# Gated mixer of a two-layer decoder: gate chains beside one value unit each, the last unit of r behind the core, head products and lower parts taking turns, the output's first unit tile by tile

## The reference, cut to what matters

```python
def gla_mixer(h, w_in, w_g2, b_g, head_norm, w_out):
    q, k, v, g_lr, r = _split(h @ w_in, ODD_SPLITS)
    gk = jax.nn.log_sigmoid((g_lr @ w_g2 + b_g).astype(jnp.float32)) / GLA_TAU
...
    G = jnp.cumsum(chunks(gk, GLA_DKH), axis=3)
    G_last = G[:, :, :, -1:, :]
    q_dec = q * jnp.exp(G)
    k_inv = k * jnp.exp(-G)
    k_rem = k * jnp.exp(G_last - G)
    att = jnp.where(tril, jnp.einsum('bnhid,bnhjd->bnhij', q_dec, k_inv), 0.0)
    o_intra = jnp.einsum('bnhij,bnhjv->bnhiv', att, v)
    def step(state, xs):
        qd, kr, vv, dec = xs
        o = jnp.einsum('bhid,bhdv->bhiv', qd, state)
        state = dec[..., None] * state + jnp.einsum('bhjd,bhjv->bhdv', kr, vv)
        return state, o
...
    o = rmsnorm(o, head_norm).reshape(Bb, S, GLA_DV).astype(h.dtype) * jax.nn.silu(r)
    return o @ w_out
```

## Time and profile before

| | us |
|---|---|
| median of 3 runs | 2367.5 (2367.14 to 2370.08) |
| the profiled execution | 2367.38 |
| its span in the profile | 2365.7 |
| PE busy | 2296.0 (97%) |
| PEld busy | 1877.5 (79%) |
| DVE busy | 1003.1 (42%) |
| ACT busy | 853.5 (36%) |
| mean granted clock of TensorE | 0.985 |

### The profile page before, as it was taken

How to read it: one execution, slowest core, us unless ns; L and a number is a source line. 1 busy time by engine, 2 the same in 40 slices (tenths; PEclk the granted TensorE clock), 3 DMA queues, 4 the chain that set the end, 5 groups by cost and what they waited for, 6 DMA issues and landing times.

```text
span 2365.7 us, 28791 instructions
## 1 busy us (share of the span) xinstructions
PE 2296.0 (97%) x10840; PEld 1877.5 (79%) x10840; DVE 1003.1 (42%) x1452; ACT 853.5 (36%) x1375; POOL 82.6 (3%) x86
## 2 busy tenths in 40 slices
PE   7999999887999999999999999999989999999999
PEld 7888888564697798888898888897758878888887
DVE  4333235687574453332353333243364545333322
ACT  4222224454554442222243222244434544323321
POOL 0000000353000000000000000000000000000000
PEclk9999999998999999999999999999999999999999
DMA  4323332121143323333322333322203521333322
GB/s 161 98 95 97 103 106 86 56 69 36 53 143 108 98 72 98 98 97 103 103 90 96 98 98 107 100 91 89 89 27 109 167 72 63 98 98 98 106 93 86
DMA packets 61939, 221.84 MB, mean 94 GB/s; under 512 B 7952, under 2 KB 8080, under 8 KB 61856
## 3 DMA queue, kind: packets, MB, share of 16 engines
q1 hardware_dynamic: 57024, 207.64, 27.7%
q10 hardware_dynamic: 4832, 13.03, 1.6%
HBM read 218.55 MB, written 2.10 MB: 93 GB/s over the span
## 4 chain that ended last, share of the span: by engine, by line
PE 93%; DVE 3%; ACT 2%; issue 1%; DMA 0%; SPq 0%; DVEq 0%; ACTq 0%
PE ps L356 18%; PE ps L358 18%; PE ps L357 18%; PE ps L1630 10%; PE ps L1632 10%; PE ps L1631 10%; PE ps L1717 1%; PE ps L1726 1%; PE ps L1531 1%; PE ps L1868 1%; PE ps L1888 1%; ACT w_hi L336 0%; DMA w_raw<-in_wstream 0%; DVE e_sc L1315 0%; PE ps L1973 0%
## 5 line engine op out<-in xcount | busy, mean ns | idle before, releaser
L356 PE MATMUL ps<-x_hi,w_hi 128*128 128x512 f32 (+1 forms) x2016 | 756.4, 375 | 4.1 <-DVE x_lo L1071 2.2
L357 PE MATMUL ps<-x_lo,w_hi 128*128 128x512 f32 (+1 forms) x2016 | 748.4, 371 | 0.0
L358 PE MATMUL ps<-x_hi,w_lo 128*128 128x512 f32 (+1 forms) x2016 | 748.1, 371 | 0.0
L341 DVE TENSOR_TENSOR w_lo<-w_raw,w_hi 128x1024 fp32r<-128x1024 f32 x194 | 241.6, 1248 | 524.9 <-ACT w_hi L336 524.4
L356 PEld LDWEIGHTS ps<-x_hi,w_hi 128*128 128x128 f32 x2016 | 382.9, 190 | 76.5 <-issue 10.5
L357 PEld LDWEIGHTS ps<-x_lo,w_hi 128*128 128x128 f32 x2016 | 383.2, 190 | 64.9 <-issue 1.4
L358 PEld LDWEIGHTS ps<-x_hi,w_lo 128*128 128x128 f32 x2016 | 382.7, 190 | 65.3
L352 DVE TENSOR_TENSOR w_lo<-w_raw,w_hi 128x1024 fp32r<-128x1024 f32 x176 | 215.7, 1226 | 291.4 <-ACT w_hi L347 291.4
L336 ACT ACTIVATE w_hi<-w_raw 128x1024 fp32r<-128x1024 f32 x194 | 204.8, 1057 | 354.3 <-PE ps L1632 276.2
L347 ACT ACTIVATE w_hi<-w_raw 128x1024 fp32r<-128x1024 f32 x176 | 186.0, 1057 | 281.0 <-PE ps L358 275.3
L1630 PE MATMUL ps<-w_hi,act_hi 128*128 128x512 f32 x608 | 236.6, 389 | 0.0
(11 more groups left out here) (280 smaller groups left out, 2249.3 us busy)
## 6 DMA issues: line engine op xcount, KB each, us to landing
w_raw<-in_wstream SPq DMA_DIRECT2D x390, 512.0 KB, 3.6
gain_bc<-in_gains ACTq DMA_DIRECT2D x8, 512.0 KB, 4.7
tmp<-in_post_gains ACTq DMA_DIRECT2D x8, 512.0 KB, 4.4
c_mem<-in_mem ACTq DMA_DIRECT2D x2, 1024.0 KB, 5.0
out_dram<-h SPq DMA_DIRECT2D x4, 512.0 KB, 2.6
h<-in_x ACTq DMA_DIRECT2D x2, 512.0 KB, 7.6
h<-in_x SPq DMA_DIRECT2D x2, 512.0 KB, 6.2
c_gain<-in_mem_gains ACTq DMA_DIRECT2D x2, 512.0 KB, 6.1
```

Of the source, the lines that this page charges most:

```text
L341: nc.vector.tensor_tensor(wl, w_raw[:, v % 2, :], wh.bitcast(f32), ALU.subtract).then_inc(w_ready, 1)
L356: nc.tensor.matmul(dst, wh, xh, start=start, stop=False)
L357: nc.tensor.matmul(dst, wh, xl, start=False, stop=False)
L358: return nc.tensor.matmul(dst, wl, xh, start=False, stop=stop)
```

## The change

Five edits, all in the gated part.

1. ACT and DVE go through the gate chains one to a value unit instead of one to two. The first three steps of chain n + 1 on ACT (`gate_log`) and the sums of chain n + 1 on DVE (`gate_sums`) stand directly behind chain n. The copy of the first value group moves behind the last chain; three weight splits follow it, the last one follows the copy of the second group.
2. The last of the eight units of r is made behind the core, in bank 6. ACT's Silu of it needs the Silu table once more. The core waits for seven units only. Its weight split (ACT and DVE) moves along: on ACT it stands ahead of the upper parts, on DVE behind all lower parts.
3. DVE makes the products of tile 0 and tile 1, then the lower parts of tile 0, the products of tile 2, the lower parts of tile 1, and so on, instead of products and lower parts of the same tile one after the other.
4. The second product of tile 0 waits for the last unit of r, the first only for the seventh.
5. The output's first unit waits before each tile for that tile's two lower parts, instead of once for all eight.

```diff
--- before.py
+++ after.py
@@ -304,6 +304,8 @@
                 return bank(6 + (t - PT0[i, "q"]) % 2)
             if parts[i][0] == "even" and t >= PT0[i, "gate"]:
                 return bank(6 + (t - PT0[i, "gate"]) % 2)
+            if parts[i][0] == "gla" and t == PT0[i, "r"] + KT - 1:
+                return bank(6)
             first = PT0[i, UNITS[parts[i][0]][0][0]]
             return bank(t - first if parts[i][0] in ("even", "gla") and t - first in (2, 3) else t % 2)
 
@@ -940,9 +942,8 @@
                 project(i, "k", GH, g_k)
                 act.wait_ge(p_free, PT0[i, "k"] + GH + 2)
                 act.preload_act_table_set("natural_log_exp_and_others")
-                for n in range(GH):
-
-                    split_units(i, "v", 1, 2 * n)
+
+                def gate_log(n):
                     act.wait_ge(gs["z"], n + 1)
                     if n > 0:
                         act.wait_ge(gs["G"], 2 * n)
@@ -951,25 +952,30 @@
                     nc.scalar.activation(tmp[:, 0, :], tmp[:, 0, :], ACT.Exp, scale=-1.0).then_inc(gs["exp"], 1)
                     act.wait_ge(gs["exp"], n + 1)
                     nc.scalar.activation(tmp[:, 0, :], tmp[:, 0, :], ACT.Ln, bias=1.0).then_inc(gs["ln"], 1)
-                    if n == 2:
-                        act.wait_ge(w_free, U[i, "v"] + 6)
-                        nc.scalar.activation(g_v[:, :, 0:SEQ], ps[:, 4:8, :], ACT.Copy).then_inc(v_ready, 1)
-
+
+                gate_log(0)
+                for n in range(GH):
+                    split_units(i, "v", 1, n)
                     act.wait_ge(gs["G"], 2 * n + 2)
                     if n > 0:
                         act.wait_ge(gs["qk"], 3 * n)
                     nc.scalar.activation(g_t[:, 0, :], tmp[:, 2, :], ACT.Exp, scale=1.0 / 16)
                     nc.scalar.activation(g_t[:, 1, :], tmp[:, 2, :], ACT.Exp, scale=-1.0 / 16).then_inc(gs["e"], 1)
                     nc.scalar.activation(tmp[:, 3, :], tmp[:, 3, :], ACT.Exp, scale=1.0 / 16).then_inc(gs["e"], 1)
-                    split_units(i, "v", 1, 2 * n + 1)
+                    if n + 1 < GH:
+                        gate_log(n + 1)
+                act.wait_ge(w_free, U[i, "v"] + 6)
+                nc.scalar.activation(g_v[:, :, 0:SEQ], ps[:, 4:8, :], ACT.Copy).then_inc(v_ready, 1)
+                split_units(i, "v", 3, GH)
                 act.wait_ge(w_free, U[i, "v"] + 10)
                 nc.scalar.activation(g_v[:, :, SEQ:2 * SEQ], ps[:, 0:4, :], ACT.Copy).then_inc(v_ready, 1)
+                split_units(i, "v", 1, KT - 1)
                 for n in range(GH):
                     act.wait_ge(gs["krT"], n + 1)
                     nc.scalar.activation(g_krt[:, :, n, :], bank(4 + n).rearrange("p (t c) -> p t c", t=TT), ACT.Copy)\
                         .then_inc(gs["krt"], 1)
                 act.preload_act_table(ACT.Silu)
-                project(i, "r", KT, g_r, func=ACT.Silu)
+                project(i, "r", KT - 1, g_r, func=ACT.Silu)
                 act.preload_act_table(ACT.Sqrt)
                 for w in range(TT * GH):
                     T, n = w // GH, w % GH
@@ -983,6 +989,8 @@
                         act.wait_ge(gs["osq"], w + 1)
                         nc.scalar.activation(g_st[:, 3, GH * T:GH * (T + 1)], g_st[:, 0, GH * T:GH * (T + 1)],
                                              ACT.Sqrt, scale=1.0 / GDV, bias=eps[:, 0:1]).then_inc(gs["root"], 1)
+                act.preload_act_table(ACT.Silu)
+                project(i, "r", KT, g_r, func=ACT.Silu, first=KT - 1)
                 for T in range(TT):
                     for b in range(2):
                         act.wait_ge(gs["y"], 2 * T + b + 1)
@@ -1409,14 +1417,13 @@
                 project(i, "q", GH)
                 project(i, "k", GH)
                 dve.wait_ge(gs["keep"], 2)
-                for n in range(GH):
-                    z = g_kr[:, n, :]
-                    split_units(i, "v", 1, 2 * n)
-
+
+                def gate_sums(n):
                     dve.wait_ge(gs["ln"], n + 1)
                     if n > 0:
                         dve.wait_ge(gs["e"], 2 * n)
-                    link(nc.vector.scalar_tensor_tensor(tmp[:, 1, :], z, 0.0, tmp[:, 0, :], ALU.min, ALU.subtract))
+                    link(nc.vector.scalar_tensor_tensor(tmp[:, 1, :], g_kr[:, n, :], 0.0, tmp[:, 0, :],
+                                                        ALU.min, ALU.subtract))
                     nc.vector.tensor_tensor_scan(tmp[:, 2, :], g_keep[:, :], tmp[:, 1, :], 0.0, ALU.mult, ALU.add)\
                         .then_inc(gs["G"], 1)
                     dve.wait_ge(gs["G"], 2 * n + 1)
@@ -1424,16 +1431,22 @@
                     nc.vector.tensor_tensor(tmp[:, 3, :].rearrange("p (c t) -> p c t", t=CH),
                                             G[:, :, CH - 1:CH].to_broadcast([P, SEQ // CH, CH]), G, ALU.subtract)\
                         .then_inc(gs["G"], 1)
-                    split_units(i, "v", 1, 2 * n + 1)
+
+                gate_sums(0)
+                for n in range(GH):
+                    split_units(i, "v", 1, n)
                     dve.wait_ge(p_free, PT0[i, "k"] + GH + 2)
                     dve.wait_ge(gs["e"], 2 * n + 2)
                     nc.vector.tensor_copy(g_dec[:, n, :],
                                           g_t[:, 0, :].rearrange("p (c t) -> p c t", t=CH)[:, :, CH - 1])
                     nc.vector.scalar_tensor_tensor(g_q[:, n, :], g_q[:, n, :], GDK ** -0.5, g_t[:, 0, :],
                                                    ALU.mult, ALU.mult).then_inc(gs["qk"], 1)
-                    nc.vector.tensor_tensor(z, g_k[:, n, :], tmp[:, 3, :], ALU.mult).then_inc(gs["qk"], 1)
+                    nc.vector.tensor_tensor(g_kr[:, n, :], g_k[:, n, :], tmp[:, 3, :], ALU.mult).then_inc(gs["qk"], 1)
                     nc.vector.tensor_tensor(g_k[:, n, :], g_k[:, n, :], g_t[:, 1, :], ALU.mult).then_inc(gs["qk"], 1)
-                project(i, "r", KT)
+                    if n + 1 < GH:
+                        gate_sums(n + 1)
+                split_units(i, "v", GH, GH)
+                project(i, "r", KT - 1)
                 dve.wait_ge(gs["qk"], 3 * GH)
                 dve.wait_ge(gs["zero"], 1)
                 dve.wait_ge(gs["mask"], 3)
@@ -1461,8 +1474,12 @@
                         normed(T - 1)
                 mean(TT - 1)
                 normed(TT - 1)
-                for T in range(TT):
+                gated(i, 0)
+                for T in range(1, TT):
                     gated(i, T)
+                    gated_lower(T - 1)
+                gated_lower(TT - 1)
+                split_units(i, "r", 1, KT - 1)
                 output(i, "out", KT // 2)
 
             def mean(T):
@@ -1489,11 +1506,13 @@
                     dve.wait_ge(gs["y_ready"], 2 * (T - 1))
                 for b in range(2):
                     dve.wait_ge(gs["oT"], 2 * T + b + 1)
-                    if T == 0 and b == 0:
-                        dve.wait_ge(p_free, PT0[i, "r"] + KT + 2)
+                    if T == 0:
+                        dve.wait_ge(p_free, PT0[i, "r"] + KT + 1 + b)
                     y = tmp[:, 2 * (T % 2) + b, :].rearrange("p (k c) -> p k c", k=4)
                     nc.vector.tensor_tensor(y, bank(2 * (T % 2) + b).rearrange("p (k c) -> p k c", k=4),
                                             g_r[:, 4 * b:4 * b + 4, T * P:(T + 1) * P], ALU.mult).then_inc(gs["y"], 1)
+
+            def gated_lower(T):
                 for b in range(2):
                     dve.wait_ge(gs["y_hi"], 2 * T + b + 1)
                     y = tmp[:, 2 * (T % 2) + b, :].rearrange("p (k c) -> p k c", k=4)
@@ -1580,7 +1599,7 @@
                     pair(2 * it + 1, 1)
                 output(i, "down", FT // 2, act_hi, act_lo)
 
-            def output(i, seg, nu, src_hi, src_lo, halves=(0, 1)):
+            def output(i, seg, nu, src_hi, src_lo, halves=(0, 1), tile_ready=None):
 
 
 
@@ -1605,6 +1624,8 @@
                             pe.wait_ge(act_ready, n0 + 2 * q + 4)
                         pe.wait_ge(w_ready, u0 + hf * nu + q + 1)
                         for t in range(TT):
+                            if tile_ready is not None and hf + q == 0:
+                                tile_ready(t)
                             last = blocks(hf, q, t)
                             if q == nu - 1 and t < TT - 1:
                                 last.then_inc(o_full, 1)
@@ -1957,9 +1978,9 @@
                                                    ident[:, :])
                     last.then_inc(gs["krT"], 1)
                 pe.wait_ge(v_ready, V0[i] + 2)
-                project(i, "r", KT, x_hi, x_lo)
+                project(i, "r", KT - 1, x_hi, x_lo)
                 pe.wait_ge(gs["krt"], GH)
-                pe.wait_ge(p_free, PT0[i, "r"] + KT + 2)
+                pe.wait_ge(p_free, PT0[i, "r"] + KT + 1)
                 pe.wait_ge(gs["qk"], 3 * GH)
 
                 def mixed(w):
@@ -1996,6 +2017,7 @@
```

(5 more changed lines are left out.)

## The result

The changed kernel took 2354.06 us (median of 5 runs, 2352.33 to 2357.64) against 2367.14 for the kernel before in the same rounds (5 runs, 2364.78 to 2370.08). The ratio is 0.9948 with a 95% interval from 0.9934 to 0.9963, that is 12.3 us less (8.8 to 15.6), clear of the 0.2% that a measurement tells. A second series gave 2352.86 against 2368.4, ratio 0.9936 (0.9920 to 0.9951), 15.2 us less. The forecast was 2351.0 with a range from 2348 to 2356: the time lies in the range, 3.1 us above the forecast.

The account below looks back on a forecast made before the run. PE bounds the kernel (on the chain for 93% of the span), so only its waits and low-clock stretches count. Gate chains 6.8 us plus behind the core 9.6 us make 16.4; 2367.4 - 16.4 = 2351.0 us, range 2348 to 2356.

Parts of the forecast that it names:

- The chains leave the path: Gate chains, at a period of 6.4 us, end more than 12 us before PE needs them; gain 6.8 us.
- C: The end of the core, at 1763.2 us in the profile before; times behind the core count from it.
- The run of 16 operations stays the bound behind the core: Behind the core, DVE's 8 products and 8 lower parts, 0.65 us each, remain the bound; the place gives 9.6 us.
- The added table load, Silu and weight split at nothing: Behind the core, Silu's table load (1.28 us), Silu (0.6) and ACT's split (1.05) hide beside other work.
- The later weight split and load at nothing: Output unit 3's split and unit 5's load go behind DVE's products, yet in time for PE; no cost.
- The clock holds: PE's clock stays up at both changed places, so the time is the summed 2351.0 us; chance 0.52.
- rival 1: Behind the moved r unit the clock falls, returning after 6.2 us of work; time 2352.0 to 2354.1 us; chance 0.30.
- D: Yardstick, set after the forecast: time from PE's first transpose of `g_kr` to ACT's first weight split inside the output.

Follow-up runs that it names:

- chains only: Against the kernel before, only the gate chains were changed, the rest left as before; median 2360.52 us, ratio 0.9969.
- without turns: The changed kernel with DVE again making each tile's lower parts right behind its products; median 2354.60 us, ratio 0.9955 against the kernel before.
- one wait: The changed kernel with one wait for all eight lower parts ahead of the output again; median 2359.32 us, ratio 0.9966 against the kernel before.

## Why the prediction was right, point by point

- **The chains leave the path.** Right, to the measured scatter: period 6.36 us (forecast 6.4), r's first matmul 4.31 us earlier relative to the transposes (4.35), the first unit of r at full clock. To C it is 84.1 us without the moved unit (as "chains only" shows), 6.6 less than before, where I had 6.8. Of these 6.6 the clock made 2.3 (forecast 2.45). Against the second profile of before it is 5.5 us, 1.2 of them the clock. The prediction took this term from one execution with a long slow stretch, and that it came out so close is in part luck.
- **The run of 16 operations stays the bound behind the core.** Right. It began at C + 6.2 (forecast C + 6.1), and ended at C + 16.1 (16.5): an operation took 0.62 us of DVE's time, not 0.65. The first unit's end was forecast at C + 18.0 on PE; PE began its second unit at 1771.97, C + 17.8.
- **The added table load, Silu and weight split at nothing.** Right: the load ended at 1756.6, PE's unit at 1759.7; DVE had no gap behind its first product. The cover of the weight split is the four products in a row: without turns DVE waits 0.37 us for it.
- **The later weight split and load at nothing.** Right: no wait of PE for weights in this stretch.
- **The clock holds** (chance 0.52), **or falls behind the r unit** (rival 1, 0.30): it held, three times of three. The measured 2354.06 sits at that rival's 2352.0 to 2354.1, but not by its mechanism. (The lower of these two is not what the rival's own working gives: 1.7 us on top of 2351.0 is 2352.7.)
- **What was off:** the sum was taken against one profiled execution, whose start and clock I took as fixed. The change gave 16.0 us in the profile against 16.4, but the first series showed 12.3; 16.4 lies above that series' interval (8.8 to 15.6) and inside the second's (11.6 to 18.9). In the profiles the difference lies ahead of the change. The last part of all twelve profiles, from the end of the output's first unit on PE to the end of the span, is the same within 0.2 us (580.3 to 580.5), and their start varies from 1670.06 to 1677.43, though the program ahead of the gated part is the same in all of them, and PE waits for nothing in the value units of any. Where that comes from shows in the attention part, 425 to 615 us, whose granted clock differs from profile to profile. The kernel with one wait and the one with only the part behind the core changed, the earliest and the latest start:

```profile
425.00:615.00 190.00, 160.96 (x616) 105.53 (x614) 144.35 (x316) 91.56 (x180) 78.52 (x67) 0.91 0.14 44
```

```profile
425.00:615.00 190.00, 160.06 (x576) 104.83 (x574) 142.47 (x305) 87.67 (x171) 78.17 (x67) 0.87 0.14 43
```

0.91 against 0.87, and 616 matmuls against 576 in the same window. A mean lower by 0.04 over 190 us is some 15 us more at half clock, which costs up to 7.6 us of work at full clock. There is a second place, beside the gates' `z`, where PE was busy throughout. The kernel before, first and second profile:

```profile
1600.00:1620.00 20.00, 20.00 (x74) 14.54 (x73) 2.52 (x3) 7.16 (x10) 0.00 (x0) 0.91 0.25 79
```

```profile
1600.00:1620.00 20.00, 20.00 (x67) 13.87 (x66) 2.45 (x2) 5.62 (x8) 0.00 (x0) 0.83 0.23 74
```

Five profiles have the 0.91 and seven the 0.83; seven matmuls of 0.23 us are 1.6 us. Over all twelve, the work that PE lost to the clock ahead of the gated part's values (its busy time times what the clock lacked of 1.00, summed in stretches of 1 us over 0 to 640 and 1590 to 1625 us) runs from 15.4 to 24.0 us, least in the profile with the earliest start and most in that with the latest. The start goes with it (correlation 0.83), but not microsecond for microsecond: the changed kernel's second profile has 22.7 and started at 1674.45, its third 20.9 and 1675.38. So the clock's placing is the best reading of the rows for the start's scatter, not shown by an experiment, and a part of the scatter stays open. The intervals of the two series (12.3 and 15.2 us less) and the 14.3 to 16.0 us in D agree with each other as well as such scatter lets them.

## What to carry to other kernels

Time a local change between two marks that enclose it, in several profiles: the changed kernel repeated D to 0.1 us, where its whole executions scattered by 10. Where an engine waits for a run of small operations, let it start on each finished piece: the tile waits gave 6.1 us of the 9.4 behind the core, of which 2.6 us were the clock that no longer fell, while the order of the small operations gave 0.8. Work moved into a wait gains at most the wait that it covers (2.3 us for a unit of 5.4 us in a wait of 3.1), and the next step is to shorten the run itself or share it with an idle engine.

## What the runs showed of the hardware

- The clock stayed up through transposes. In the changed kernel PE did 32 of them, and one matmul, between 1759.7 and 1764.1 us, busy 4.04 of 4.40 us, and the granted clock stayed at 1.00 there and after, in three profiles. The Trainium skill, TensorE: Matmul & The Clock Gate, Part 4, says that a transpose doesn't count as PE-busy in the same way; these profiles speak against it for fp32 transposes of 128x128, but don't settle it, since the dense r unit ends only 4.5 us ahead of the output's first matmul. The strongest row is that of "one wait": 32 transposes from 1754.2 to 1758.6, nothing behind them, and the clock fell 8.9 us after the r unit, where in "chains only", with 16 transposes in a block and then nothing, it fell 4.0 us after the core. Before the change, with as many transposes but gaps of 2.6 and 1.5 us between them, the clock fell.
- A busy PE is not enough to keep the clock. Beside the eight matmul records of `z`, which have 16 rows where the others have 128, it fell to 0.50 in all twelve profiles while PE was busy for 20 of 20 us; in the profile of before it was low from 1605.5 to 1608.9. Whether it is the 16 rows that do it was not tested.
- The clock falls at places that differ from one execution to the next, and so does the time back at half speed: in two profiles of the same kernel 5.1 and 2.5 us at the start of r, 6.2 and 4.7 us at the output.
- A subtraction of two SBUF tiles on DVE took 1.14 us instead of 0.69 with the same kind on POOL beside it for all its time; a product that reads PSUM on DVE kept its 0.65. Of the two on POOL that it overlapped by 0.6 us each, the first took 1.28 us, the second 1.75, where 1.27 was the time in the attention part. The Trainium skill, GPSIMD Engine Reference, Specifications, names SBUF interfaces shared with VectorE and contention with DVE instructions that have two SBUF inputs; for DVE these rows agree. POOL's third subtraction took 1.60 us though DVE's products stood beside it for most of its time, so it isn't shown that only such pairs cost POOL time.
